# Input in column parts between the first weights, small loads moved to one queue, differential keys copied out at once, and last chunks taken earlier, in a two-block transformer kernel

## What is computed

```python
def first_block(x, ...):
    h = rmsnorm(x, norm_mix_pre)
    m = mixer(h, w_in, b_f, conv_w, w_branch, w_out)   # forgetting attention + gated convolution
    x = x + rmsnorm(m, norm_mix_post)
    h = rmsnorm(x, norm_ffn_pre)
    return x + rmsnorm(swiglu(h, w_gate_up, w_down), norm_ffn_post)

def second_block(x, mem, ...):
    x = x + 0.5 * swiglu_2(rms_norm(x, norm_ffn1), ffn1_w1, ffn1_w3, ffn1_w2)
    x = x + hybrid_mixer(rms_norm(x, norm_mix), w_in, ...)   # retention + differential attention
    x = x + memory_attention(rms_norm(x, norm_mem_q), rms_norm(mem, norm_mem_kv), ...)
    x = x + 0.5 * swiglu_2(rms_norm(x, norm_ffn2), ffn2_w1, ffn2_w3, ffn2_w2)
    return rms_norm(x, norm_out)
```

## Time and profile before

| | before |
|---|---|
| time, median of three runs | 1004.46 us |
| the profiled execution's own time | 1004.28 us |
| its span in the trace | 1002.4 us |
| PE busy with matmuls | 980.0 us (98% of the span), 5804 instructions |
| DVE busy | 676.9 us (68%) |
| ACT busy | 496.5 us (50%) |
| transfers | 176.26 MB, 176 GB/s on average |

### The profile page before, as it was taken

The page is one execution under the profiler, slowest core; times in us unless marked ns, Lnnn a source line. Parts: engine busy times, 40 slices in busy tenths (PEclk is TensorE's granted clock), DMA queues, the critical chain, the costliest instruction groups (busy, mean ns, idle before and its releaser), DMA issues.

```text
span 1002.4 us, 14420 instructions
## 1 busy us (share of the span) xinstructions
PE 980.0 (98%) x5804; PEld 867.9 (87%) x5804; DVE 676.9 (68%) x686; ACT 496.5 (50%) x658; POOL 16.7 (2%) x20
## 2 busy tenths in 40 slices
PE   7999999999999999999999999899999999999996
PEld 7999999888888888888888888798999878888885
DVE  3646867767777766877777776485664576777776
ACT  5354654773343444844343446374865554343433
POOL 0000000013000000000000000000000000000000
PEclk9999999999999999999999999999999999999999
DMA  9655474564655555555656545543445345656551
GB/s 290 190 161 160 152 272 143 195 204 129 208 195 197 194 188 188 171 197 178 209 167 209 167 169 195 160 150 126 163 132 189 104 148 168 209 167 209 167 168 42
DMA packets 126118, 176.26 MB, mean 176 GB/s; under 512 B 4010, under 2 KB 102524, under 8 KB 125948
## 3 DMA queue, kind: packets, MB, share of 16 engines
q1 hardware_dynamic: 123980, 172.28, 52.0%
q10 hardware_dynamic: 2096, 3.38, 1.1%
HBM read 174.60 MB, written 1.05 MB: 175 GB/s over the span
## 4 chain that ended last, share of the span: by engine, by line
PE 84%; DVE 8%; ACT 4%; issue 2%; DMA 1%; SPq 0%; ACTq 0%; DVEq 0%
PE up_banks L562 11%; PE gate_banks L562 10%; PE bank L413 8%; PE bank L414 8%; PE bank L415 8%; PE up_banks L413 7%; PE up_banks L414 7%; PE up_banks L415 7%; PE up_banks L567 6%; PE gate_banks L567 5%; DVE w_lo L1500 3%; ACT w_hi L994 2%; DMA stage<-in_w_in 1%; DVE gate L1619 1%; PE bank L496 1%
## 5 line engine op out<-in xcount | busy, mean ns | idle before, releaser
L1506 DVE TENSOR_TENSOR w_lo<-stage,w_hi 128x2048 fp32r<-128x2048 f32 x81 | 185.4, 2289 | 96.5 <-ACT w_hi L1001 96.5
L1500 DVE TENSOR_TENSOR w_lo<-stage,w_hi 128x2048 fp32r<-128x2048 f32 x79 | 180.7, 2294 | 92.0 <-ACT w_hi L994 92.0
L994 ACT ACTIVATE w_hi<-stage 128x2048 fp32r<-128x2048 f32 x79 | 150.5, 1911 | 66.6 <-PE up_banks L415 47.8
L1001 ACT ACTIVATE w_hi<-stage 128x2048 fp32r<-128x2048 f32 x81 | 153.0, 1905 | 0.0
L413 PE MATMUL up_banks<-act_both,w_hi 128*128 128x256 f32 x480 | 138.9, 289 | 1.8 <-DVE act_both L1513 1.3
L414 PE MATMUL up_banks<-act_both,w_hi 128*128 128x256 f32 x480 | 136.7, 285 | 0.0
L415 PE MATMUL up_banks<-act_both,w_lo 128*128 128x256 f32 x480 | 136.6, 285 | 0.0
L562 PE MATMUL gate_banks<-act_both,w_hi 128*128 128x512 f32 x528 | 135.4, 393 | 0.0
L562 PE MATMUL up_banks<-act_both,w_hi 128*128 128x512 f32 x528 | 132.6, 393 | 0.0
L562 PEld LDWEIGHTS up_banks<-act_both,w_hi 128*128 128x128 f32 x528 | 97.1, 189 | 18.6
L562 PEld LDWEIGHTS gate_banks<-act_both,w_hi 128*128 128x128 f32 x528 | 93.8, 189 | 15.8
(11 more groups left out here) (332 smaller groups left out, 1437.7 us busy)
## 6 DMA issues: line engine op xcount, KB each, us to landing
stage<-in_ffn_w SPq DMA_DIRECT2D x66, 1024.0 KB, 5.3
stage<-in_w_in SPq DMA_DIRECT2D x33, 1024.0 KB, 5.3
stage<-in_w_gate_up SPq DMA_DIRECT2D x22, 1024.0 KB, 5.1
stage<-in_w_down SPq DMA_DIRECT2D x11, 1024.0 KB, 4.9
stage<-in_w_out SPq DMA_DIRECT2D x8, 1024.0 KB, 4.9
stage<-in_mem_w_kv SPq DMA_DIRECT2D x8, 1024.0 KB, 5.0
stage<-in_w_branch SPq DMA_DIRECT2D x4, 1024.0 KB, 6.0
stage<-in_mem_w_q SPq DMA_DIRECT2D x4, 1024.0 KB, 5.2
```

Of the source, the lines that this page charges most:

```text
L994: act.activation(w_hi[:, place, :], stage[:, place, :], copy).then_inc(hi_done, 1)
L1001: act.activation(w_hi[:, place, :], stage[:, place, :], copy).then_inc(hi_done, 1)
L1500: dve.tensor_tensor(w_lo[:, place, :], stage[:, place, :], w_hi[:, place, :].bitcast(F32), ALU.subtract).then_inc(lo_done, 1)
L1506: dve.tensor_tensor(w_lo[:, place, :], stage[:, place, :], w_hi[:, place, :].bitcast(F32), ALU.subtract).then_inc(lo_done, 1)
```

## The change

In the code, seven things move. (1) x is loaded in two halves of its columns, each ahead of its half of chunk 0; constants, `wf` and the table go from ACT's queue to SP's, between chunks; PE transposes one half of x, runs six matmuls on zeros, transposes the other and runs fourteen. (2) ACT squares x only after `hi(1)`, and loads the root's table earlier. (3) The first factor rows are made in the middle of the product of chunk 1; DVE does chunk 2 before the first queries. (4) The key product is done in one piece, with the queries' sums behind it. ACT copies each key tile out of PSUM right after squaring it, so `DK` joins `BY_ACT`, the chunks whose banks ACT frees, and DVE scales the copy. (5) `hi(last)` stands ahead of the last silu in all three feed-forwards. (6) `lo(111)` stands behind the first of two differences. (7) Ahead of the third feed-forward, the table load is earlier, two of the four squares stand between the two halves of `gained`, and `lo(129)` stands behind the diagonal.

```diff
-            for t in range(2):
-                sp.dma_start(x_n[:, t, :], a["x"][0, t * P:t * P + P, :]).then_inc(x_landed, 16)
             for half, done in enumerate((half_landed, landed[0])):
+                cols = slice(512 * half, 512 * half + 512)
+                for t in range(2):
+                    sp.dma_start(x_n[:, t, cols], a["x"][0, t * P:t * P + P, cols]).then_inc(x_landed[half], 16)
                 sp.dma_start(stage[:, 0, half * CH // 2:(half + 1) * CH // 2].rearrange("p (k n) -> p k n", k=KD // 2),
...
-            wholes(Q + 1, w_in, 256, 2)
+            wholes(Q + 1, w_in, 256, 1)
+            sp.dma_start(const[:, P:C_END], a["consts"][:, P:C_END]).then_inc(const_landed, 16)
+            wholes(K, w_in, 256 * 2, 1)
+            sp.dma_start(wf[:, :, :], w_in.rearrange("(k p) n -> p k n", p=P)[:, :, 1536:1544]).then_inc(wf_landed, 16)
             parameters(sp)
             wholes(K + 1, w_in, 256 * 3, 1)
             token_pair(V, w_in, 1024)
+            for r in range(0, P, 32):
+                sp.dma_start(sel[r:r + 32, :, :], a["consts"][0:32, C_END:C_END + 1024].rearrange("p (h m) -> p h m", h=8)
+                             ).then_inc(table_landed, 16)
...
-            for _ in range(12):
-                pe.matmul(bank[AUX][:, 0:P], idle, idle, start=True, stop=True)
+            for half in range(2):
+                pe.wait_ge(x_landed[half], 32)
...
+                for _ in range(6 + 8 * half):
+                    pe.matmul(bank[AUX][:, 0:P], idle, idle, start=True, stop=True)
+
+            def first_factors():
+                pe.wait_ge(const_landed, 16)
+                factor_rows(0, SUM)
...
-            pe.wait_ge(const_landed, 16)
             pe.wait_ge(gain_done, 1)
-            factor_rows(0, SUM)
-            up(Q + 1, act_hi, act_lo)
+            up(Q + 1, act_hi, act_lo, between=first_factors)
...
-            up_tok(DK, act_hi, act_lo, 0)
+            tokens(DK, act_hi, act_lo)
...
-            up_tok(DK, act_hi, act_lo, 1)
...
-                wait_read(pe, DK + t)
+                pe.wait_ge(kn_done, t + 1)
...
                 hi(last - 1)
+                hi(last)
                 hidden(PAIRS - 2, 1)
-                hi(last)
...
-            def diff_key_squares(t):
-                act.activation(k_sq[t], token_result(act, DK, t), ACT.Square).then_inc(ksq_done, 1)
+            def diff_key_in(t):
+                src = token_result(act, DK, t)
+                act.activation(k_sq[t], src, ACT.Square).then_inc(ksq_done, 1)
+                act.activation(k_n[t], src, copy).then_inc(up_free_act, 1)
...
-            gained(par, G_FFN2, 5, MEMQ + 4)
-            warm(ACT.Sqrt)
-            squares(N_FFN2, S_FFN2)
+            gained(par, G_FFN2, 5, MEMQ + 4, range(0, 4))
+            squares(N_FFN2, S_FFN2, range(0, 2))
+            gained(par, G_FFN2, 5, 0, range(4, KD))
+            squares(N_FFN2, S_FFN2, range(2, 4))
...
-            lo(2)
+            dve.wait_ge(zeroed, 6)
             lo(3)
             query(Q + 1)
+            dve.wait_ge(wf_hi_done, 1)
+            dve.tensor_tensor(wf_lo4, wf4, wf_hi4.bitcast(F32), ALU.subtract).then_inc(wf_lo_done, 1)
...
-            lo(129)
             mean_square(N_FFN2)
             inverse(N_FFN2)
             spread(N_FFN2)
+            lo(129)
```

More of the change, by code:

```diff
@@ L211, in build @@
         DIFF_OUT, RET_OUT = (ACC + 3, SUM), (SUM, AUX)
-        x_landed, const_landed, par_landed = sem("x_landed"), sem("const_landed"), sem("par_landed")
+        x_landed = [sem(f"x_landed{i}") for i in range(2)]
+        const_landed, par_landed = sem("const_landed"), sem("par_landed")
         ident_landed = sem("ident_landed")
@@ L435, in up_product @@
                     for m in range(2):
+                        if between is not None and m:
+                            between()
                         for k in range(KD):
@@ L635, in _ @@
             pe.transpose(bank[SUM][:, 0:KD], first_rows[:, :], ident[0:KD, 0:KD]).then_inc(gain_turned, 1)
[L636 to L642, removed]
-            for _ in range(12):
-                pe.matmul(bank[AUX][:, 0:P], idle, idle, start=True, stop=True)
+            for half in range(2):
+                pe.wait_ge(x_landed[half], 32)
+                for b in (2 * half, 2 * half + 1):
+                    for m in range(2):
+                        for t in range(2):
+                            d0 = (2 * b + m) * P
+                            mm = pe.transpose(pair[ACC + b][:, m, t * P:t * P + P], x_n[:, t, d0:d0 + P], ident)
+                    mm.then_inc(x_turned, 1)
+                for _ in range(6 + 8 * half):
[3 more added lines that the diff above has]
+                factor_rows(0, SUM)
             pe.wait_ge(half_lo_done, 1)
             up_product(pair[UP], 0, act_hi, act_lo, act_lo_done, 0, halves=True)
-            pe.wait_ge(const_landed, 16)
             pe.wait_ge(gain_done, 1)
-            factor_rows(0, SUM)
-            up(Q + 1, act_hi, act_lo)
+            up(Q + 1, act_hi, act_lo, between=first_factors)
             pe.wait_ge(par_landed, 16 * 24)
@@ L1095, in _ @@
             act.dma_start(first_rows[:, :], a["norm_mix_pre"][0].rearrange("(k p) -> k p", p=P)).then_inc(gain_landed, 16)
[L1096 to L1101, removed]
             act.wait_ge(idle_ready, 1)
             act.activation(diag[:, 0, 0:1], idle[:, 0:1], copy)
-            act.wait_ge(x_landed, 32)
-            for q in range(2):
-                square(N_X0, q, of_x(x_n, q))
             first, second = slice(0, CH // 2), slice(CH // 2, CH)
             act.wait_ge(gain_done, 1)
-            gained(first_gain, 0, 0, 0, range(0, 2))
+            gained(first_gain, 0, 0, 0, range(0, 4))
             act.wait_ge(half_landed, 16)
             act.activation(w_hi[:, 0, first], stage[:, 0, first], copy).then_inc(half_hi_done, 1)
-            gained(first_gain, 0, 0, 0, range(2, 4))
+            gained(first_gain, 0, 0, 0, range(4, KD))
             act.wait_ge(landed[0], 16)
             act.activation(w_hi[:, 0, second], stage[:, 0, second], copy).then_inc(hi_done, 1)
-            gained(first_gain, 0, 0, 0, range(4, KD))
-            for q in range(2, 4):
+            act.wait_ge(zeroed, 6)
+            warm(ACT.Sqrt)
+            hi(1)
+            for q in range(4):
                 square(N_X0, q, of_x(x_n, q))
-            hi(1)
+            deviation(N_X0)
+            hi(2)
+            rows_out(N_X0, SUM)
+            hi(3)
             act.wait_ge(wf_landed, 16)
-            act.wait_ge(zeroed, 6)
             act.activation(wf_hi4, wf4, copy).then_inc(wf_hi_done, 1)
-            warm(ACT.Sqrt)
-            deviation(N_X0)
-            rows_out(N_X0, SUM)
-            hi(2)
-            hi(3)
             hi(4)
@@ L1306, in _ @@
             hi(106)
+            hi(107)
+            diff_key_in(0)
+            diff_key_in(1)
+            diff_key_deviation(0)
+            diff_key_deviation(1)
             act.wait_ge(aux_done, A_DQ + 1)
-            act.wait_ge(teps_done, 1)
             for t in range(2):
@@ L1656, in half_lo @@
                                   ).then_inc(done, 1)
+            gained(first_gain, 0, 0, range(0, 4))
             half_lo(slice(0, CH // 2), half_hi_done, half_lo_done)
-            gained(first_gain, 0, 0, range(0, 4))
+            gained(first_gain, 0, 0, range(4, KD))
             half_lo(slice(CH // 2, CH), hi_done, lo_done)
-            gained(first_gain, 0, 0, range(4, KD))
             lo(1)
-            dve.wait_ge(wf_hi_done, 1)
-            dve.wait_ge(zeroed, 6)
-            dve.tensor_tensor(wf_lo4, wf4, wf_hi4.bitcast(F32), ALU.subtract).then_inc(wf_lo_done, 1)
             mean_square(N_X0)
             inverse(N_X0)
+            dve.wait_ge(ident_landed, 16)
             spread(N_X0)
+            lo(2)
             dve.wait_ge(rs_done, 1)
```

27 lines of the change are left out of this document (11 added, 16 removed).

## The result

The changed kernel takes 993.35 us as a median of four runs (992.18 to 993.60), the kernel before 1004.42 beside it: a ratio of 0.9889, 95% interval 0.9877 to 0.9902. Forecast were 992.6 us and a range of 990.5 to 998.0. The profiled execution took 993.32 us, its span is 991.3.

A forecast was written before the change was run, and what follows sets the result against it. PE was busy 980.0 of 1002.4 us, so only its waits and slowdowns could be won. Start 4.4 + keys 3.0 + ends 2.1 + third feed-forward 2.4 = 11.9; 1004.28 - 11.9 = 992.4, as median 992.6 us, range 990.5 to 998.0.

The forecast's parts named there:

- the five waits: PE's wait entries: first diagonal 3.7, key tile 3.0, third feed-forward's diagonal 2.2, `last_lo` three times 0.7, first product 1.3 us.
- the two that it announced: New PE waits: about 1.2 us before chunk 3 for DVE's small products, 1.4 for `w_lo` at 813.
- the start: Up to chunk 3: PE starts its product at 32.45 instead of 36.8 us, a gain of 4.4 us.
- the ends: Feed-forward ends: `last_lo` comes up to 2.5 us sooner, PE needs it only 0.7 sooner; three times, 2.1 us.
- the keys: Key product: ACT's copy frees the bank, so the next product starts unhindered; the wait of 3.0 us is gained.
- PEclk is 1.00 throughout: Sign for the whole kernel: no slow clock; a clock of 0.50 anywhere before the end would be wrong.
- its argument from the 1.3: Third feed-forward: 1.4 us of idling is about the 1.3 that kept the clock at the start, so it is kept.
- chunk 3 late with the clock down: Rival at the start: the start gives about 0, total gain 7.5, time 997.0 us; chance 0.14.
- not each wait has that price: PE's waits: clock 0.69 behind the 3.7 us wait, 0.77 behind the 2.2, but 1.00 behind the 3.0.
- Third feed-forward: Ahead of it: PE resumes 0.9 us sooner, plus 1.7 of clock kept, less 0.2 given back: 2.4 us.
- `lo(111)`, 0 forecast: Between the two differences: costs and gives nothing, since DVE does the same work to the second one's end.
- The rival built on its holding the queue for 9.9 us: SP's queue: `wf` holds it, PE starts chunk 3 at 39.4, total gain 2.5, 1002.0 us; chance 0.04.

The follow-up runs named there:

- with zeros in it: Changed kernel with six matmuls on zeros put into PE's wait ahead of chunk 3: 991.93 us.
- the ends alone: Kernel before with one edit, ACT copying the last chunk ahead of the last silu in each feed-forward: 1002.31 us, ratio 0.9980.
- the run without `wf`: Changed kernel with `wf` alone issued from ACT's queue again, as before the change: 989.68 us.
- the start alone: Kernel before with only the edits of SP's queue, PE, ACT and DVE up to chunk 4, and `up_product`'s `between`: 1003.09 us, ratio 0.9985.
- the version with none over 1.0: Changed kernel with `wf` on ACT's queue, DVE's parameters before `lo(3)`, `lo(129)` in halves, and ten instead of fourteen zero matmuls before chunk 0's product: 988.13 us.
- The keys alone: Kernel before with only the key edits (both halves in one product, ACT copies them out, DVE scales the copy): 1000.97 us, ratio 0.9969.

## Why the prediction was right, and where it was off

The time came out 0.75 us above the forecast, and mostly for the forecast's reasons: the five waits are gone, the two that it announced are there, at their places and nearly at their lengths. Two terms were off, in opposite directions: the start gave 2.2 less than forecast, the ends 1.0 and the keys 0.3 more. That the total comes as close as 0.75 us is partly luck. Chunk 106's product, forecast near 635.0, started at 636.2: 2.2 less from the start, 0.7 more from two ends, 0.3 more from the keys.

- **Start, 4.4 forecast, 2.2 in the profile.** Its chain was right in each link: the zeros cover the first wait, the diagonal is off the path, `wf` makes a second hold on SP's queue (3.0 forecast for it; 2.5 and 3.3 by the run without it), and DVE's order makes PE wait. Landing and start came 0.65 us later. The step that failed is the price of that new wait: the sum puts no slow clock behind its 1.2 us, and the signs say "PEclk is 1.00 throughout", without a reason given in that part. The prediction had read four waits, 1.3 and 3.0 us with the clock kept, 2.2 and 3.7 with it lost; its argument from the 1.3 is made only for the third feed-forward. The wait is 1.6 to 2.3 us, and behind it the clock fell in three of five profiles and cost 1.5 to 1.6 us; with zeros in it, it didn't. The rival "chunk 3 late with the clock down" was half right: the clock without the lateness.
- **Ends, 2.1 forecast, 3.1 measured.** The step was "PE needs it only 0.7 sooner". A wait's length in the table is not its price: with the lost overlap each cost 1.0, by the three places of the table above; the median of the ends alone (2.2) doesn't show it. The same holds for the keys, 3.0 forecast and 3.3 measured.
- **Third feed-forward, 2.4 forecast, 2.5 measured**, in its parts too: 0.9 us sooner, a wait of 1.2 (forecast 1.4), and 1.5 from the clock kept behind it (forecast 1.7 less 0.2). That the clock is kept there was a guess from one row; seven profiles bear it out.
- **`lo(111)`, 0 forecast**, and none found.
- The prediction read the clock's fall as a property of a wait: "not each wait has that price". The runs say it more exactly: not each execution has it. The 2.4 us behind the first wait and the 1.7 behind the 2.2 were real in the execution that was read, and the other terms of the sum would have been smaller or larger by as much in another one.
- The small load: `wf` took 11.1 us from issue to landing on SP's queue. The estimate of 10.8 us takes the figure of about 10.5 ns per packet in the Trainium skill, "DMA: Bandwidth & Descriptors", section Bandwidth, for each of its 1024 lines. The trace's number is near it but doesn't bear the working out: chunk 3, with 1024 lines too, lands in 5.5 us, and chunk 2, issued 0.6 us ahead of `wf` on the same queue, takes 11.5 and lands 0.2 us ahead of it. So a wait behind chunk 2 explains the landing as well. The rival built on its holding the queue for 9.9 us doesn't follow: the queue was held for 3.7, and by the run without `wf` that hold comes even to a row in its place.

## What to carry to other kernels

On an engine that is busy 98% of the time, a wait costs its length and about 0.3 us of lost overlap, and, behind 12 of the 17 waits of 1.6 us and more here, another 1.5 us or so of slow clock; a forecast should carry that last part as a chance and a spread, not as a yes or no. A small load with many lines is better kept off the queue that carries the next large one, and small work that doesn't need that load should stand ahead of it in the engine's order. Where medians of single edits don't add up to the whole, look in the traces for a wait that the single edit leaves in place and that now costs more.

## What the runs showed of the hardware that was not expected

- The same wait of PE, 3.0 us at the same instruction, was followed by a granted clock of 1.00 in two profiles and of 0.76 to 0.78 over 7 us in two. Of 17 waits between 1.6 and 4.2 us, 12 had a slow stretch behind them; of seven waits of 1.24 us, and of seven of 1.2 to 1.6 us before the first product, none.
- A PEclk of 0.76 over 7 us is 1.7 us of full clock lost; behind the longest waits, 3.7 to 4.2 us, it was 0.61 to 0.76, a loss of up to 2.7. The runs of one kernel tend to spread with the waits left in it: 1000.05 to 1004.97 us for the start alone, with waits of 2.1, 3.0 and 2.2 us left in it, 987.22 to 988.56 for the version with none over 1.0. The keys alone, with 4.2 and 2.2 left and runs within 0.8 us, don't follow that.
- The load issued right behind chunk 2, with 1 MB loads in flight ahead of it, is held in SP's queue for 3.4 to 4.0 us, whether it is `wf` (32 KB in 1024 lines, seven profiles) or one parameter row (3.7 to 3.9, four profiles). Behind `wf` the next row is held 2.8 to 3.6 us more; behind the row the next one isn't. Taking `wf` off the queue brought chunk 3's issue forward by 2.5 to 3.3 us.
